# A transformer layer with a routed MoE on one core: x2 kept in SBUF, a third down buffer elsewhere, a refill in quarters, a 32-row expert last, row gathers split

## The chip, the cores and the metric

One core of one Trainium2 chip. The metric is device microseconds of one execution, lower is better. Engines: TensorE (PE), VectorE (DVE), ScalarE (ACT), GpSimd (POOL) and SyncE (SP). SP, ACT and POOL issue the DMAs of this kernel.

## The reference, cut to what matters

One layer over 512 tokens of width 1024 in float32. The mixer half (four kinds of heads and an output projection) gives `x2`. The second half is a mixture of 16 experts (4 groups of 4). A token takes its best group, and in it its two best experts:

```
h  = adaLN(rms_norm(x2), c)
p_group = softmax(h @ w_rg + b_rg);  g = argmax(p_group)
p_exp   = softmax(logits of the 4 experts of group g); two best: e1, e2
y  = p_group[g] * sum over e in (e1, e2) of p_e/(p_e1+p_e2) * ((silu(h @ w_gate[e]) * (h @ w_up[e])) @ w_down[e])
x3 = x2 + gate(c) * y;   out = rms_norm(x3) * final_norm
```

Each expert has w_gate and w_up of 1024 x 512 and w_down of 512 x 1024, 2 MB each, so the 16 experts are 96 MB of weights that each pass through SBUF once. Which tokens an expert gets is known only after the routing.

## The kernel before, in words

The first 390 us (mixer, attention, delta rule) are not touched by the change. Four output projections (L1131), one per 128 tokens, give `x2` [128, 4, 1024] in SBUF. From each block DVE makes the normalised rows `xn2`, which SP stores to HBM (`xn2_rows`, L931), and PE the 20 routing logits.

**Routing (dve_moe, pe_moe).** DVE picks group and experts by a long chain of small linked operations, up to `chosen` (tokens x experts, L1351). PE forms each token's rank within its expert with one matmul by `before` and four by `ones` (L1187, L1191). DVE turns the ranks of experts 0 and 1 into one-hot rows (`in_row`, L1359), PE multiplies both by the token numbers (L1198), and DVE copies both token lists at once (L1369). Then DVE orders the other experts by their number of tokens: `size` is an expert's position. After that come the first row of each position's tile in the output buffer (`tile0`), the surplus tiles beyond an expert's own, and the slot of each token in `expert_rows` (L1371 to L1428).

**Experts.** Position n of the run works on `ORDER[n]`. The tile heights by position in the ordering are `SIZES` = 8 of 128 rows, 4 of 64, 4 of 32. The order in which the tiles run is 0, 1, 2, 15, 3, 14, 4, 13, 5, 12, 6, 11, 7, 8, 9, 10: the last three have 64 rows. Up to 12 extra tiles of 128 rows, taken only if an expert has too many tokens, follow behind `If`s (`extras`). Each expert is: POOL gathers its rows from `xn2_rows` (L1491); PE transposes them (L987); ACT and DVE scale them into `xgT` (L1059, L1089); PE does gate and up (L1018 for 128 rows, L1012 for fewer); ACT the silu (L1066), DVE the product `hidm` (L1097, L1099); PE transposes it (L1026), ACT copies it to `hidT` (L1071); PE does down (L1049, L1044); DVE multiplies by the gate into the one buffer `yo` (L1114, L1110) and ACT stores it to `expert_rows` (L1081). DVE writes `yo` of expert n only when all stores of expert n-1 have landed. On PE the order is: hidden transposes of n-1, gate and up of n, row transposes of n+1, down of n-1. On ACT the store of expert n-1 comes before the copy of the next `hidT`.

**Weights.** Three buffers each: `gu0` to `gu2` (gate and up, 4 MB) and `dn0` to `dn2` (down, 2 MB). SP issues the loads in program order: gu0 and gu1 during attention, dn0 and dn1 after the last output projection, then the four stores of `x2` to HBM (L936), gu2, and dn2 behind a wait for those stores, as `dn2` lies on the memory of `x2`. From then on the buffer of expert n is refilled when expert n is done with it: for n = 3 to 15 gate and up wait for `gu_mm` (L952 in the file, shown as L896, the helper that issues them), down for `dn_mm` (L899). At the end SP loads `fnb` and then `x2` back from HBM as `x3` (L961).

**Tail.** When the last expert's rows have landed, POOL passes the 12 `If`s of the extra tiles and gathers the rows of each token: `y1` and `y2` in turn for the four token blocks (L1512). DVE adds `w1 * y1` (L1467) and `w2 * y2` (L1468) into `x3`, block after block, with the final norm of a block (L1478) after the next block's two additions. ACT gives the sums of squares and roots (L1285, L1287), SP stores the four blocks (L973).

```
ORDER = list(range(NBUF))
big, less = list(range(NBUF, BIG)), list(range(BIG, E))
rest = less[::-1] if NBUF == 3 else less
while big:
    ORDER.append(rest.pop(0))
    ORDER.append(big.pop(0))
ORDER += rest[::-1] if NBUF == 3 else rest
```

Of the kernel before, what the change touches and what calls it, by code (L numbers as in the profile page):

```python
# [32 lines left out]
for _n, _w in IN_SIZES.items():  # L33
# [17 lines left out]
ROUTING = {"chosen": 1, "first_rows": 2, "second_rows": 3, "first_list": 4, "experts": 5, "places": 6, "slots": 7,  # L51
           "list": 8, "w12": 9, "route_i": 10}
ROUTING_PE = {"rank_mm": 1, "first_list_mm": 2, "list_mm": 3}
SIZES = [128] * 8 + [64] * 4 + [32] * 4
TILE_START = [sum(SIZES[:n]) for n in range(E + 1)]
TILE_START += [TILE_START[E] + P * (n + 1) for n in range(EXTRA - 1)]
ROWS = TILE_START[-1] + P
# [19 lines left out]
def sbuf_map(nc):  # L77
# [55 lines left out]
    at("dn2", R1 + 64 * K + 256, [P, FT, D])  # L133
    at("x3", RW + 16 * K, [P, ST, D])
# [44 lines left out]
    for n, shape in (("lg", [P, ST, 20]), ("mx", [P, ST]), ("mn", [P, ST]), ("m1", [P, ST]), ("ed", [P, ST]),  # L179
                     ("t4", [P, ST, 4]), ("eg", [P, ST, 4]), ("ohg", [P, ST, 4]), ("oh1", [P, ST, 4]),  # L180
                     ("oh2", [P, ST, 4]), ("le", [P, ST, 4]), ("e16", [P, ST, E]), ("s16", [P, ST, E]),
                     ("M1", [P, ST, E]), ("M2", [P, ST, E]), ("chosen", [P, ST + 1, E]), ("rank", [P, ST, E]),
# [21 lines left out]
    o = at("idf", o, [P, P])  # L204
# [14 lines left out]
    o = at("vc", o, [P, HD])  # L219
    o = at("wr", o, [P, KT, 20])  # L220
# [24 lines left out]
def build(nc, A, out):  # L245
# [623 lines left out]
    x2_d = nc.dram_tensor("x2_rows", [S, D], F32).ap()  # L869
# [7 lines left out]
    big, less = list(range(NBUF, BIG)), list(range(BIG, E))  # L877
# [23 lines left out]
    def sync_moe(sp):  # L901
# [33 lines left out]
        for i in range(ST):  # L935
            sp.dma_start(x2_d[i * P:(i + 1) * P, :], T["x2"][:, i, :]).then_inc(sem("x2_st"), 16)  # L936
# [6 lines left out]
        sp.wait_ge(sem("x2_st"), 16 * ST)  # L943
        load_down(sp, 2, 2)
        sp.wait_ge(sem("routing"), ROUTING["experts"])
        expert = {}
        for n in range(NBUF, E + 1):

            if n < E:
                at_rank = 1 + EXTRA + ORDER[n]  # L950
                expert[n] = sp.value_load(T["route_i"][0:1, at_rank:at_rank + 1], min_val=0, max_val=E - 1)
                sp.wait_ge(sem("gu_mm"), n - NBUF + 1)  # L952
                load_gate_up(sp, expert[n], n % NBUF)
# [6 lines left out]
        sp.wait_ge(sem("dn_mm"), E - 2)  # L960
        sp.dma_start(T["x3"][:], x2_d.rearrange("(i p) d -> p i d", p=P)).then_inc(sem("x3_in"), 16)  # L961
# [9 lines left out]
        for i in range(ST):  # L971
            sp.wait_ge(sem("final"), i + 1)
            sp.dma_start(out[0, i * P:(i + 1) * P, :], T["x3"][:, i, :]).then_inc(sem("out_st"), 16)  # L973
# [26 lines left out]
    def pe_gate_up(pe, n, b):  # L1000
        w_in = gu[buffer_of(n)]
        pe.wait_ge(sem(f"gu_in{buffer_of(n)}"), 32 * loads_of(n))
# [114 lines left out]
    def extras(eng, body):  # L1117
# [30 lines left out]
    def pe_moe(pe):  # L1148
# [34 lines left out]

        pe.wait_ge(sem("routing"), ROUTING["chosen"])
        ch = T["chosen"]
        rank = PS[6][:, 0:(ST + 1) * E]
        t.matmul(rank, T["before"][:], ch[:].rearrange("p i e -> p (i e)"), start=True, stop=False)  # L1187
        for i in range(1, ST + 1):

            n = ST + 1 - i  # L1190
            ins = t.matmul(PS[6][:, i * E:(ST + 1) * E], T["ones"][:], ch[:, 0:n, :].rearrange("p i e -> p (i e)"),  # L1191
                           start=False, stop=(i == ST))
        ins.then_inc(sem("routing_pe"), 1)

# [1219 lines left out]
```

## Time and profile before

| | us |
|---|---|
| median of 3 runs | 793.02 (789.85, 793.02, 796.32) |
| the profiled execution | 793.18 |
| its span, first to last instruction | 791.3 |
| outside the span | 1.88 |
| PE busy in the span | 683.7 (86%) |
| DVE, ACT, POOL busy | 313.4, 179.5, 118.3 |
| HBM read, written | 159.21 MB, 18.36 MB |

All times of the trace are microseconds from the span's start. A DMA's duration in the timeline is the time to issue it; its landing is told separately. "Granted clock" is TensorE's clock as a share of full speed (1.00 is 2.4 GHz, 0.50 is 1.2 GHz). A row `x16` in the timeline is 16 neighbouring instructions; a float32 matmul shows as two.

### The profile page before, as it was taken

How to read it: one execution, taken by the hardware profiler on the slowest of the kernel's cores; microseconds unless marked ns; L12 is line 12 of the kernel's file. 1: busy time of each engine (PE TensorE's matmuls, PEld its weight loads, DVE VectorE, ACT ScalarE, POOL GpSimd, SP SyncE). 2: the span in 40 equal slices, each digit the busy share in tenths (PEclk: the TensorE clock that was granted, in tenths of full speed). 3: DMA queues.
4: the chain of work that ended last, by engine and by line, in shares of the span. 5: the costliest groups of instructions: out<-in, count | busy, mean ns of one | idle time of the engine just before them, and what ended most of it. 6: DMA issues, size and time to landing. Idle time of an engine off the chain costs nothing.

```text
span 791.3 us, 9785 instructions
## 1 busy us (share of the span) xinstructions
PE 683.7 (86%) x3805; PEld 397.5 (50%) x3809; DVE 313.4 (40%) x730; ACT 179.5 (23%) x434; POOL 118.3 (15%) x164
## 2 busy tenths in 40 slices
PE   2699899999999998889999953999999999899720
PEld 1574446667675797555544443444454454344200
DVE  3203757767566433776522256331211111111107
ACT  3204225121111212456411141111121121111103
POOL 8600123213050273000000001000000000000031
PEclk9789999999999999889999965999999999999965
DMA  9999003983320302640261099168999999999945
GB/s 332 375 261 348 3 0 107 278 253 107 107 106 1 56 2 96 183 202 1 73 194 53 28 335 382 72 277 328 407 407 426 404 398 422 370 411 411 411 164 223
DMA packets 74065, 178.31 MB, mean 225 GB/s; under 512 B 21954, under 2 KB 38940, under 8 KB 69916
## 3 DMA queue, kind: packets, MB, share of 16 engines
q1 hardware_dynamic: 67968, 161.78, 55.8%
q0 software_dynamic: 2816, 9.96, 3.4%
q10 hardware_dynamic: 3228, 5.84, 2.0%
q8 instruction: 36, 0.59, 0.3%
q14 instruction: 17, 0.14, 0.1%
HBM read 159.21 MB, written 18.36 MB: 224 GB/s over the span
## 4 chain that ended last, share of the span: by engine, by line
PE 69%; DMA 11%; DVE 9%; POOL 4%; ACT 3%; issue 3%; SPq 1%; POOLq 0%; ACTq 0%; DVEq 0%
PE ps L1018 13%; DMA gu<-in_w_up 9%; PE ps L1131 7%; PE ps L2239 7%; PE ps L2206 5%; PE ps L1049 4%; PE ps L1012 3%; PE ps L2317 2%; PE ps L2323 2%; PE ps L2203 2%; PE ps L2230 2%; PE ps L1044 2%; POOL lev L1587 2%; PE ps L2327 2%; PE ps L652 1%
## 5 line engine op out<-in xcount | busy, mean ns | idle before, releaser
L1018 PE MATMUL ps<-gu,xgT 128*128 128x512 f32 x256 | 116.0, 612 | 5.1 <-ACT xgT L1059 2.8
L1018 PEld LDWEIGHTS ps<-gu,xgT 128*128 128x128 f32 x256 | 49.7, 197 | 67.4 <-issue 64.8
L1491 POOL DMA_INDIRECT xg<-xn_rows,list x16 | 14.9, 930 | 387.1 <-PE ps L987 181.6
L2239 PE MATMUL ps<-hT,winr 128*128 128x512 f32 x144 | 72.3, 610 | 0.2
L1049 PE MATMUL ps<-dn,hidT 128*128 128x512 f32 x128 | 56.5, 594 | 0.0
L1131 PE MATMUL ps<-wout,yT 128*128 128x512 f32 x128 | 55.9, 595 | 0.0
L1692 POOL TENSOR_TENSOR cc<-low,lev 128x512 f32<-128x512 f32 x20 | 30.2, 1517 | 129.5 <-DVE low L2026 104.1
L1830 DVE SCALAR_TENSOR_TENSOR acc<-ada,st,acc 128x512 f32<-128x512 f32 x56 | 48.5, 866 | 1.3
L1012 PE MATMUL ps<-gu,xgT 128*32 128x256 f32 (+1 forms) x384 | 43.0, 452 | 2.2 <-DMA gu<-in_w_up 2.2
L2206 PE MATMUL ps<-hT,wind 128*128 128x512 f32 x96 | 42.3, 593 | 0.0
L1099 DVE TENSOR_TENSOR hidm<-sg,ps 128x512 f32<-128x512 f32 x8 | 5.5, 686 | 90.3 <-ACT sg L1066 90.3
L1131 PEld LDWEIGHTS ps<-wout,yT 128*128 128x128 f32 x128 | 24.0, 190 | 28.9 <-issue 28.9
L1049 PEld LDWEIGHTS ps<-dn,hidT 128*128 128x128 f32 x128 | 23.7, 190 | 26.9 <-issue 26.8
L1066 ACT ACTIVATE sg<-ps 128x512 f32<-128x512 f32 (+2 forms) x16 | 7.4, 464 | 128.0 <-PE ps L1018 102.5
L2239 PEld LDWEIGHTS ps<-hT,winr 128*128 128x128 f32 x144 | 23.8, 190 | 14.3 <-issue 12.3
L1012 PEld LDWEIGHTS ps<-gu,xgT 128*32 128x32 f32 (+1 forms) x384 | 16.7, 119 | 24.5 <-issue 17.2
L1114 DVE TENSOR_TENSOR yo<-ps,g2m 128x512 f32<-128x512 f32 x16 | 10.3, 686 | 46.4 <-PE ps L1049 27.8
L2125 PE MATMUL ps<-ada,st 128*32 128x128 f32 x256 | 11.6, 347 | 19.1 <-DMA ada<-in_w_ada 18.0
L1059 ACT ACTIVATE xgT<-ps,st 128x128 f32<-128x128 f32 (+2 forms) x64 | 21.9, 423 | 27.1 <-PE ps L987 26.6
L2206 PEld LDWEIGHTS ps<-hT,wind 128*128 128x128 f32 x96 | 17.8, 190 | 20.2 <-issue 20.1
L726 DVE TENSOR_REDUCE st<-ps 128x1 f32<-128x256 f32 (+3 forms) x48 | 20.3, 452 | 18.3 <-PE ps L659 18.1
L1071 ACT ACTIVATE hidT<-ps 128x512 f32<-128x512 f32 (+2 forms) x16 | 7.4, 464 | 86.6 <-DVE yo L1114 59.8
(414 smaller groups left out, 1054.2 us busy)
## 6 DMA issues: line engine op xcount, KB each, us to landing
gu<-in_w_gate SPq DMA_DIRECT2D x16, 2048.0 KB, 17.2
gu<-in_w_up SPq DMA_DIRECT2D x16, 2048.0 KB, 22.3
dn<-in_w_down SPq DMA_DIRECT2D x16, 2048.0 KB, 25.2
ada<-in_w_ada SPq DMA_DIRECT2D x12, 2048.0 KB, 11.7
expert_rows<-zero SPq DMA_DIRECT2D x12, 512.0 KB, 7.1
expert_rows<-yo ACTq DMA_DIRECT2D x8, 512.0 KB
wout<-in_w_out SPq DMA_DIRECT2D x1, 3072.0 KB, 10.6
x<-in_x SPq DMA_DIRECT2D x2, 1024.0 KB, 6.7
```

The costliest lines, as they stand in the source:

```text
L726: ins = v.tensor_reduce(m, PS[n][:, 0:nk], AX.X, ALU.max, negate=True)
L1012: ins = nc.tensor.matmul(PS[2 * b][m * s:m * s + m, 0:2 * f].rearrange("p (w f) -> p w f", w=2), T["xgT"][:, k, 0:m], w_in[:, :, k, s * f: ...
L1018: ins = nc.tensor.matmul(PS[2 * b + w][:, :], T["xgT"][:, k, :], w_in[:, w, k, :], start=(k == 0), stop=(k == KT - 1))
L1044: ins = nc.tensor.matmul(PS[4][m * w:m * w + m, 0:d], T["hidT"][:, c, m * s:m * s + m], w_in[:, f, w * d:(w + 1) * d], start=(f == 0), sto ...
L1049: ins = nc.tensor.matmul(PS[4 + w][:, :], T["hidT"][:, f, :], w_in[:, f, w * 512:(w + 1) * 512], start=(f == 0), stop=(f == FT - 1))
L1059: ins = nc.scalar.activation(T["xgT"][:, k, 0:m], PS[6][:, k * m:(k + 1) * m], ACT.Identity, scale=rA[:, k:k + 1], bias=rshift[:, k:k + 1])
L1131: ins = nc.tensor.matmul(PS[2 * (i % 2) + n][:, :], T["yT"][:, k, i * P:(i + 1) * P], T["wout"][:, k, n * 512:(n + 1) * 512], start=(k == ...
L1587: link(g.affine_select(out=t, in_=t, pattern=pattern, compare_op=op, fill=fill, base=base, channel_multiplier=cm))
L1692: g.tensor_tensor(CC[lv % 2][:], T["low"][:], T["lev"][:, lv].unsqueeze(1).broadcast_to([P, H, P]), ALU.mult).then_inc(sem("cc"), 1)
L1830: ins = v.scalar_tensor_tensor(o, piece[:, k, :], csil[:, k:k + 1], o, ALU.mult, ALU.add)
L2206: ins = t.matmul(bank[:, :], w(k), T["hT"][:, k, :], start=(k == 0), stop=(k == KT - 1))
L2239: ins = t.matmul(bank[:, :], w(k), T["hT"][:, k, :], start=(k == 0), stop=(k == KT - 1))
```

## The change

- `x2` stays in SBUF: it isn't stored to HBM nor loaded back, the tail works on it in place. `dn2` moves to memory of constants and buffers that are dead by then, and is loaded right behind dn0 and dn1, after the last output projection.
- The first refill of gate and up (buffer 0, for n = 3) comes in four parts of two k-steps each, each when expert 0's matmuls have passed these steps. 8 DMAs instead of 2.
- The order of the tiles ends with one of 32 rows: 0, 1, 2, 14, 3, 13, 4, 12, 5, 11, 6, 10, 7, 9, 8, 15. So positions 9 and 15 of the run have 64 and 32 rows where they had 32 and 64. The tile of the last expert stands at the end of `expert_rows`, which takes two more DVE operations in the routing.
- DVE forms `earlier` (chosen experts summed over earlier blocks, four linked additions), and PE forms the ranks with two matmuls instead of five.
- The lists of expert 0 and 1 go into two banks with a signal each, and POOL's gather for expert 0 waits for the first list alone.
- For a token one of whose experts is the last one, `y1` and `y2` and their weights are exchanged where needed so that `y1` never lies in the last tile. The four `y1` gathers wait only for the stores of the first 15 experts, and stand ahead of the extras' `If`s; the four `y2` gathers come last. DVE adds all four `w1 * y1` when all four have landed, then goes on by blocks with `w2 * y2`.

```diff
+OTHER_ROWS = sum(SIZES[:E - 1]) + P * EXTRA
+TILE_START += [OTHER_ROWS] + [sum(SIZES[:E - 1]) + P * n for n in range(EXTRA)]
...
-    at("dn2", R1 + 64 * K + 256, [P, FT, D])
-    at("x3", RW + 16 * K, [P, ST, D])
+    at("dn2", o2, [P, FT, D])
...
-    rest = less[::-1] if NBUF == 3 else less
+    big, less = list(range(NBUF, BIG)), list(range(E - 2, BIG - 1, -1))
     while big:
-        ORDER.append(rest.pop(0))
+        ORDER.append(less.pop(0))
         ORDER.append(big.pop(0))
-    ORDER += rest[::-1] if NBUF == 3 else rest
+    ORDER += less + [E - 1]
...
                 for b in range(2):
                     load_down(sp, b, b)
+                sp.wait_ge(sem("yo_zero"), 16 * EXTRA)
+                load_down(sp, 2, 2)
...
-        for i in range(ST):
-            sp.dma_start(x2_d[i * P:(i + 1) * P, :], T["x2"][:, i, :]).then_inc(sem("x2_st"), 16)
         sp.wait_ge(sem("g2_moved"), 1)
...
         load_gate_up(sp, 2, 2)
-        sp.wait_ge(sem("x2_st"), 16 * ST)
-        load_down(sp, 2, 2)
...
+                if n == NBUF:
+                    for part in range(4):
+                        if part < 3:
+                            sp.wait_ge(sem("first_gu_mm"), part + 1)
+                        else:
+                            sp.wait_ge(sem("gu_mm"), 1)
+                        ks = slice(2 * part, 2 * part + 2)
+                        for w, view in enumerate((wg_v, wu_v)):
+                            sp.dma_start(gu[0][:, w, ks], view[expert[n]][:, ks]).then_inc(sem("gu_in0"), 16)
+                else:
+                    sp.wait_ge(sem("gu_mm"), n - NBUF + 1)
+                    load_gate_up(sp, expert[n], n % NBUF)
...
-        sp.wait_ge(sem("dn_mm"), E - 2)
-        sp.dma_start(T["x3"][:], x2_d.rearrange("(i p) d -> p i d", p=P)).then_inc(sem("x3_in"), 16)
...
         t.matmul(rank, T["before"][:], T["chosen"][:].rearrange("p i e -> p (i e)"), start=True, stop=False)
-        for i in range(1, ST + 1):
-            n = ST + 1 - i
-            ins = t.matmul(PS[6][:, i * E:(ST + 1) * E], T["ones"][:], ch[:, 0:n, :].rearrange("p i e -> p (i e)"),
-                           start=False, stop=(i == ST))
-        ins.then_inc(sem("routing_pe"), 1)
+        t.matmul(rank, T["ones"][:], T["earlier"][:].rearrange("p i e -> p (i e)"), start=False,
+                 stop=True).then_inc(sem("routing_pe"), 1)
...
+        link(v.tensor_tensor(T["chosen"][:, 0:ST], T["M1"][:], T["M2"][:], ALU.add))
+        for i in range(1, ST + 1):
+            ins = v.tensor_tensor(T["earlier"][:, i, :], T["earlier"][:, i - 1, :], T["chosen"][:, i - 1, :], ALU.add)
...
-        v.tensor_copy(T["list"][:, 0:2], PS[5][:, 0:2]).then_inc(sem("routing"), 1)
+        v.tensor_copy(T["list"][:, 0:1], PS[4][:, 0:1]).then_inc(sem("routing"), 1)
+        dve.wait_ge(sem("routing_pe"), ROUTING_PE["second_list_mm"])
+        v.tensor_copy(T["list"][:, 1:2], PS[5][:, 0:1]).then_inc(sem("routing"), 1)
...
+        link(v.tensor_scalar(t16, order, E - 1.5, float(OTHER_ROWS - sum(SIZES[:E - 1])), ALU.is_gt, ALU.mult))
+        link(v.tensor_tensor(tile0, tile0, t16, ALU.add))
...
+        swap, move = T["mx"][:], T["mn"][:]
+        link(v.tensor_scalar(t16, order, float(LAST), None, ALU.is_equal))
+        link(v.tensor_tensor(T["s16"][:], T["M1"][:], t16.unsqueeze(1).broadcast_to([P, ST, E]), ALU.mult))
+        link(v.tensor_reduce(swap, T["s16"][:], AX.X, ALU.add))
+        for one_of, two in ((w1, w2), (T["slotf"][:, 0, :], T["slotf"][:, 1, :])):
+            link(v.tensor_tensor(move, two, one_of, ALU.subtract))
+            link(v.tensor_tensor(move, move, swap, ALU.mult))
+            link(v.tensor_tensor(one_of, one_of, move, ALU.add))
+            link(v.tensor_tensor(two, two, move, ALU.subtract))
+        v.tensor_copy(T["slot"][:], T["slotf"][:]).then_inc(sem("routing"), 1)
...
+        dve.wait_ge(sem("y1_in"), 16 * ST)
+        with dve.If(n_extra > 0):
+            dve.wait_ge(sem("y1_in"), 2 * 16 * ST)
+        for i in range(ST):
+            x = T["x2"][:, i, :]
+            ins = v.scalar_tensor_tensor(x, T["y1"][:, i, :], w1[:, i:i + 1], x, ALU.mult, ALU.add)
+        link(ins)
...
-                link(v.scalar_tensor_tensor(x, y, w1[:, c], x, ALU.mult, ALU.add))
...
+        pool.wait_ge(sem("routing"), ROUTING["slots"])
+        pool.wait_ge(sem("yo_st"), 16 * STORED[E - 1])
+        for i in range(ST):
+            rows_back(0, "y1_in", i)
+        n_extra = extras(pool, extra)
+        with pool.If(n_extra > 0):
+            pool.wait_ge(sem("y1_in"), 16 * ST)
+            for i in range(ST):
+                rows_back(0, "y1_in", i)
         pool.wait_ge(sem("yo_st"), 16 * STORED[E])
-        pool.wait_ge(sem("routing"), ROUTING["slots"])
-        extras(pool, extra)
         for i in range(ST):
-            for n, y in enumerate(("y1", "y2")):
-                g.indirect_dma_start(T[y][:, i, :], None, yo_d,
-                                     at(ap=T["slot"][:, n, i:i + 1], axis=0)).then_inc(sem(f"y_in{i}"), 16)
+            rows_back(1, f"y_in{i}", i)
```

## Rows read from the trace of the kernel before

**Rows 1.** The page, part 2: DMA's busy tenths in 40 slices of 19.8 us.
```profile
DMA  9999003983320302640261099168999999999945
```

**Rows 2.** The chain that ended last: start, length, engine and operation.
```profile
480.37 8.50 DMA xg<-xn_rows,list
492.58 16.80 PE ps L1018 x32
...
705.06 32.94 DMA gu<-in_w_up
...
757.56 2.87 DMA expert_rows<-yo
```

**Rows 3.** Windows of 5 us: busy time by engine, granted clock, DMA share, GB/s.
```profile
500.00:505.00 5.00, 5.00 (x13) 2.16 (x12) 0.00 (x0) 0.00 (x0) 0.00 (x0) 1.00 0.00 0
520.00:525.00 5.00, 5.00 (x13) 2.16 (x12) 0.00 (x0) 0.00 (x0) 0.00 (x0) 1.00 0.54 220
545.00:550.00 5.00, 5.00 (x19) 2.20 (x17) 0.00 (x0) 0.38 (x1) 0.00 (x0) 1.00 0.55 225
740.00:745.00 5.00, 5.00 (x26) 1.62 (x24) 0.00 (x0) 0.00 (x0) 0.00 (x0) 1.00 1.03 413
```

**Rows 4.** Timeline of the routing: start, length, engine, line, idle before it.
```profile
461.64 0.34 SPq L931 DMA_DIRECT2D xn_rows<-xn  x1
471.70 0.71 PE L1187 MATMUL ps<-chosen,before 128*128 128x80 f32 x2 [6.13 <-DVE chosen L1351]
472.21 1.81 PE L1191 MATMUL ps<-chosen,ones 128*128 128x64 f32 x8
475.32 3.57 PE L1198 MATMUL ps<-tok,in_row 128*128 128x1 f32 x16 [1.30 <-DVE in_row L1359]
479.35 0.16 DVE L1369 CAST list<-ps 128x2 uint32<-128x2 f32 x1 [2.28 <-PE ps L1198]
487.99 0.06 DVE L1408 MEMSET yo<- 128x1 f32 x1
```

**Rows 5.** Groups by line, 452 to 792 us: a small DVE operation, mean 175 ns.
```profile
L1441 DVE TENSOR_SCALAR t<-incl 128x16 f32<-128x16 f32 x12 | 2.1, 175 | 0.4
```

**Rows 6.** DMA issues, 455 to 475 us: size, us to landing.
```profile
xn_rows<-xn SPq DMA_DIRECT2D x1, 512.0 KB, 9.7
```

**Rows 7.** Timeline of PE in the experts: down and gate/up by rows.
```profile
640.34 1.93 PE L1044 MATMUL ps<-dn,hidT 128*32 128x256 f32 x32
...
642.79 3.66 PE L1012 MATMUL ps<-gu,xgT 128*32 128x256 f32 x64
...
671.21 7.09 PE L1012 MATMUL ps<-gu,xgT 128*64 128x512 f32 x32
...
688.75 15.70 PE L1018 MATMUL ps<-gu,xgT 128*128 128x512 f32 x32 [2.34 <-DMA gu<-in_w_up]
...
735.36 0.44 PE L1026 MATMUL ps<-idf,hidm 128*128 128x128 f32 x2
...
750.98 5.27 PE L1044 MATMUL ps<-dn,hidT 128*64 128x512 f32 x16 [2.04 <-ACT hidT L1071]
```

**Rows 8.** Timeline, stores of `yo` and the tail (first row: ACT, a 32-row expert).
```profile
586.07 1.75 ACTq L1081 DMA_DIRECT2D expert_rows<-yo  x4
...
725.39 0.34 ACTq L1081 DMA_DIRECT2D expert_rows<-yo  x1
...
736.37 0.69 DVE L1110 TENSOR_TENSOR yo<-ps,g2s 128x512 f32<-128x512 f32 x1 [3.26 <-DMA expert_rows<-yo]
...
763.76 0.94 POOL L1512 DMA_INDIRECT y<-expert_rows,slot  x1 [57.50 <-issue]
...
771.22 1.72 POOL L1512 DMA_INDIRECT y<-expert_rows,slot  x1 [0.31 <-issue]
772.16 1.28 DVE L1468 SCALAR_TENSOR_TENSOR x<-y,w2t,x 128x1024 f32<-128x1024 f32 x1
```

**Rows 9.** The tile `y`: time from issue to landing of its 8 gathers.
```profile
DMA to landing us min/median/max: 4.3/5.9/6.7
```

More of the change, by code:

```diff
@@ L50 @@
 NBUF = 3
-ROUTING = {"chosen": 1, "first_rows": 2, "second_rows": 3, "first_list": 4, "experts": 5, "places": 6, "slots": 7,
-           "list": 8, "w12": 9, "route_i": 10}
-ROUTING_PE = {"rank_mm": 1, "first_list_mm": 2, "list_mm": 3}
+ROUTING = {"before_tile": 1, "first_rows": 2, "second_rows": 3, "first_list": 4, "second_list": 5, "experts": 6,
+           "places": 7, "list": 8, "w12": 9, "slots": 10, "route_i": 11}
+ROUTING_PE = {"rank_mm": 1, "first_list_mm": 2, "second_list_mm": 3, "list_mm": 4}
 SIZES = [128] * 8 + [64] * 4 + [32] * 4
-TILE_START = [sum(SIZES[:n]) for n in range(E + 1)]
-TILE_START += [TILE_START[E] + P * (n + 1) for n in range(EXTRA - 1)]
-ROWS = TILE_START[-1] + P
+TILE_START = [sum(SIZES[:n]) for n in range(E - 1)]
+OTHER_ROWS = sum(SIZES[:E - 1]) + P * EXTRA
+TILE_START += [OTHER_ROWS] + [sum(SIZES[:E - 1]) + P * n for n in range(EXTRA)]
+ROWS = OTHER_ROWS + SIZES[E - 1]
 BIG = SIZES.count(P)
@@ L219, in sbuf_map @@
     o = at("vc", o, [P, HD])
+    o = at("acc1", o, [P, 512])
+    o = at("wpool", o, [P, 2, HD])
+    at("dn2", o2, [P, FT, D])
+    assert o2 + 16 * K <= o
+    o = at("idf", o, [P, P])
+    o = at("cols", o, [P, P])
+    o = at("ones", o, [P, P])
+    o = at("before", o, [P, P])
     o = at("wr", o, [P, KT, 20])
@@ L1001, in pe_gate_up @@
         w_in = gu[buffer_of(n)]
-        pe.wait_ge(sem(f"gu_in{buffer_of(n)}"), 32 * loads_of(n))
+        pe.wait_ge(sem(f"gu_in{buffer_of(n)}"), 32 * loads_of(n) + (96 if n >= NBUF and not buffer_of(n) else 0))
         pe.wait_ge(sem("xgT_a"), n + 1)
@@ L1314, in dve_moe @@
         lg = T["lg"]
-        link(v.memset(T["chosen"][:, ST, :], 0.0))
+        v.memset(T["chosen"][:, ST, :], 0.0)
+        link(v.memset(T["earlier"][:, 0, :], 0.0))
         link(v.tensor_tensor(T["rb"][:], T["rb"][:], PS[7][:, 80:100], ALU.add))
@@ L1455, in extra @@
             dve_output(dve, n)
-        extras(dve, extra)
+        n_extra = extras(dve, extra)
+        dve.wait_ge(sem("y1_in"), 16 * ST)
[4 more added lines that the diff above has]
+            ins = v.scalar_tensor_tensor(x, T["y1"][:, i, :], w1[:, i:i + 1], x, ALU.mult, ALU.add)
+        link(ins)
         dve.wait_ge(sem("fn_in"), 16)
-        dve.wait_ge(sem("x3_in"), 16)
-        dve.wait_ge(sem("routing"), ROUTING["w12"])
         for i in range(ST + 1):
@@ L1472, in dve_moe @@
             i -= 1
[L1473 removed]
+            c, x = slice(i, i + 1), T["x2"][:, i, :]
             dve.wait_ge(sem("ss"), 2 * ST + i + 1)
@@ L1494, in pool_moe @@
         for n in range(E):
-            if n == 2:
-                pool.wait_ge(sem("routing"), ROUTING["list"])
+            if n in (1, 2):
+                pool.wait_ge(sem("routing"), ROUTING[("second_list", "list")[n - 1]])
             if n >= 2:
```

48 lines of the change are left out of this document (23 added, 25 removed).

## The prediction, made before the changed kernel ran

> **What bounds the kernel now.** I read the page's slices first [rows 1]: in the last third, from about 545 us on, the DMA row stands at nine tenths or more until slice 38, while before it there are idle slices. The chain that ended last [rows 2] says the same in other words. It runs over PE from 492.58 on, and in the last hundred microseconds over two waits for gate/up weights, of which the longer shown takes 32.94 us and ends at 738.0, where PE starts the last expert's gate/up. From there on it is a plain sequence: the last expert, its store, the row gathers, the final norm. The windows [rows 3] date the start of the saturation: DMA is at share 0.00 in 500 to 505, at 0.54 in 520 to 525, at 0.55 in 545 to 550, and then full. The third window's end is where expert 2's gate/up matmuls end and free their buffer. So there are three stretches. (1) Up to about 550 the time goes by the routing and by PE on experts 0 to 2. (2) From 550 to 738 DMA moves weights without a gap at some 413 GB/s [rows 3]. (3) From 738 to 791.3 comes the tail of 53.3 us. What moves the start of (1) moves all behind it, since the stream of (2) starts when PE has freed the buffers; inside (2) only bytes count; in (3) each step counts.
>
> **Stretch 1: the routing.** The five rank matmuls take 471.70 to 474.02 [rows 4]. Two of width 80 take 0.71 plus about 0.45 (a quarter of the 1.81 us of the other four): 1.16 instead of 2.32, so 1.16 less. Against this DVE adds four linked additions of 175 ns [rows 5], with the link about 0.21 each: 0.84 more. Net 0.3 earlier. Bounds: 1.2 earlier to 0.8 later.
>
> The first list is the larger part. The matmuls of both lists run 475.32 to 478.89, the first list's half ends at 477.1, less the 0.3 is 476.8. DVE copied both lists 0.46 after PE's end [rows 4]; now it copies the first at 477.3, and is free by then. POOL's gather started 1.0 after that copy did (480.37 after 479.35), so now at 478.3, 2.1 earlier. If its landing takes the 8.5 us of before [rows 2], all follows 2.1 earlier, and PE starts expert 0 at 490.5 instead of 492.58.
>
> Two things stand close behind. DVE must also have finished its chain before it scales expert 0's rows: it did at 488.05 [rows 4]. Now the chain starts 0.3 earlier, has one more copy and two more linked operations (0.42 and 0.2), and so ends at 488.3. The rows' transposes would end at about 488.8, so DVE doesn't bind yet, but caps the gain at 2.1 + 0.6 = 2.7. The other is the `xn2` store. It was issued at 461.64 and took 9.7 us [rows 4, 6], so landed at 471.3, behind dn0 and dn1 (4.2 MB). Now dn2, 2.1 MB, stands ahead of it as well: 2.1 MB at 413 GB/s is 5.1 us, landing at 476.4, still ahead of the first gather at 478.3 with 1 to 2 us to spare. gu2's load moves from 471.4 to 476.5 behind it and is not needed before expert 2. It shares the DMA engines with the gather as the backlog did before, which is why I keep 8.5; without any backlog it could be the 4.3 to 6.7 of [rows 9], and then the DVE cap of 2.7 holds. Value 2.1 earlier, bounds 2.7 earlier to 2 later.
>
> The trace shows the `xn2` store at 9.7 us behind two loads of its queue [rows 6]. The Trainium skill (DMA: Bandwidth & Descriptors, section Queues, rings and completion order) says that each engine takes its descriptors of one queue in ring order and takes turns between queues. The trace agrees. By this rule the store waits for all of dn2, which is the 5.1 us above; by a free sharing of the engines it would be nothing, and both leave the gather where it is.
>
> **Stretch 2: the stream.** The refill in quarters starts gu's first refill when 2 of 8 k-steps are done, some 12 us earlier. That fills the window that shows share 0.00 [rows 3], but nothing waits for this load: the next refill waits for expert 1's matmuls, dn3 for expert 0's down, and DMA is idle again at 520 to 525 and 545 to 550. I cost it at nothing; what hides it is that idle time. Bounds: 0 to 1 gained. Its six extra issues lie on SP while SP has nothing else to issue. The four stores of `x2` lay ahead of the gather, in time that the routing covers; the load of `x3` was issued at the very end of the stream, behind all weights. So the 4.2 MB saved shorten no part of (2). The stream's end, the last gate/up load, moves by stretch 1 alone: 738.04 - 2.1 = 735.9.
>
> PE must not be later than that. Position 9 of the run now has 64 rows: 7.09 against 3.66 for gate/up [rows 7], and for down 3.65 or so (five sevenths of 5.27, of which a part ran at 1.2 GHz) against 1.93. That is 5.2 us more. PE waited 2.34 us before position 12 [rows 7] and 2.24 us before position 15 (from 735.8 to 738.04). The first wait absorbs 2.3, so position 12 starts 2.9 later; it ran 15.70 with a part at the lower clock after its wait, which without the wait falls away, some 1.8. PE is then ready for position 15 at 735.8 + 2.9 - 1.8 - 2.1 = 734.8, before the weights. If the clock part stays, it is 736.6, 0.7 after them. I take 0, bounds 0 to 0.8 lost.
>
> **Stretch 3: the tail.** Times are from the new 735.9. Gate/up of 32 rows takes 3.66, to 739.5. The down weights of the expert before land 2.1 MB later, 5.1 us, at 741.0: a new wait of 1.5. Down of 64 rows, 3.65: 744.7. DVE could write `yo` at 744.9, but needs the previous store landed. Such a store was issued at 725.39, and DVE waited for it until 736.37 [rows 8]: 11 us in the full stream. The one in question is issued at about 736.4, so lands by that at 747.4; but the stream behind it has only 5 MB left. I take the middle, 746.2 (bounds 744.9 and 747.4). Then 0.69 for DVE, some 1.1 for ACT's two issues (four take 1.75 [rows 8]), an estimated 0.3 for `hidT`: 748.4. Down of 32 rows takes 1.93 at full clock [rows 7]; the last one of before ran 5.27 after a wait of 2.04 where 3.65 is the full-speed value, so I take 3.4 (bounds 1.9 and 3.9): 751.8. DVE and the four issues of 1.75 [rows 8] bring 754.1, and 2.87 more to land [rows 2]: 757.0.
>
> `y1` needs the store of the expert before, issued by 748.0 and landed about 750.4. So POOL starts `y1` at 750.8. Each gather takes 0.94 and a gap of 0.3 [rows 8]: 755.8. Then the 12 `If`s. They cost 763.76 - 760.43 = 3.3 us on the path before [rows 2, 8] and stand now between `y1` and `y2`: `y2` starts at 759.1, after the last store (757.0). Its first block lands 5.9 later [rows 9], 765.0. All four `y1` have landed 3.7 + 5.9 = 9.6 after the first issue, 760.4; DVE adds them in 4 x 1.28 = 5.1 [rows 8]: 765.6. So DVE binds, narrowly. Block 0 is ready at 765.6 + 1.3 = 766.9; before it was 772.16 + 1.28 = 773.44 [rows 8]. From there 17.86 us remained. Two of the following steps had a `w1` product inside, 2 x 1.28 = 2.6 less (the third overlaps ACT's table load and roots): 15.3. The span ends at 782.2. Over all: stretch 1 gives 2.1, the tail 53.3 - 46.3 = 7.0. With the 1.9 outside the span, 784.1, against 793.18 of the profiled run, which is the median of 793.02.
>
> Before, one gather took 1.72 instead of 0.94 while DVE added rows [rows 8]. The Trainium skill (SBUF — State Buffer, section Who interferes with whom) says that a DVE instruction with two SBUF inputs and a GpSimd instruction that reads SBUF exclude each other. By it each `y2` gather issued under the four `w1` products may take up to 1.3 more; by most rows it takes nothing. DVE uses a block only every 3 us, so the last block would be late by under 1 us in the worst case.
>
> DVE's 12 operations for the exchange of weights and slots (2.5 us) fall in the stretch before the silu of expert 1, where DVE is idle, as in 520 to 525 [rows 3]. If that cover were gone, expert 1's product would be late by as much. Bounds 0 to 1.
>
> **The rivals.**
> - *The front gives nothing.* The `xn2` store lands later than 478 behind dn2, or the gather meets gu2's load at its densest. For it: a slack of only 1 to 2 us. Against: 5.1 us is all that dn2 holds. The gather lands 1 us later than before: 784.1 + 3.1 = 787.2.
> - *More than forecast.* The stream gains from the early refill, or the gather lands early, or the store of position 13 lands in time. For it: 1.3 us in that store, 0.6 at the DVE cap, 1.6 if `y1` lands in 4.3 [rows 9]. Against: PE can start the last expert only at 734.8, so the stream can give 1.1 at most. Time 781.
> - *Slower: the split gathers hang on a late store.* Each store of `yo` lands 11 us after its issue [rows 8] even as the stream runs out, one behind the other. Then the store of position 14 is issued from 748.1 to 749.2 and lands at 760.5; `y1` starts at 761 instead of 750.8, and the three serial pieces behind it (9.6, 5.1 and 16.6 us) end the span at 792.3, time 794.2, 1 us slower than before. It decides from a start of `y1` at 759.9 on. Against: the stream is empty from about 747, and a store in empty queues took 2.87 [rows 2].
> - *PE binds in the stream* by position 9's 64 rows: 784.9, within the forecast's own range.
>
> **How the numbers follow.** The forecast 784.1 has 0.50 with its own range 781.5 to 787; the front gives nothing 0.17; more than forecast 0.23; the late store 0.06; 0.04 for what I don't see. The bounds of the parts add to 780.6 at best, and with the scatter of the runs to 778.5; upwards to the first rival and some of the third, 790.5. About 1% (785.1) is what a measurement can tell from no change. Below it lie six tenths of the forecast's case, nearly all of the better one: 0.55 faster. The late store alone is within 1%; slower by more takes it together with the lost front (797), or what I don't see: 0.04. Within: 0.41.
>
> **What would show it.** Right: the first gather issued near 478 and expert 0's matmuls near 490.5; a refill between 494 and 508 with DMA idle again before 525; saturation from about 548; gate/up of the last expert near 736; `y1` gathers from about 751 and `y2` about 3.3 us after their end; four additions in a row on DVE. Wrong: a wait of the first gather for `xn_rows`; last weights landing well ahead of 735; `y1` starting after 757; a wait of PE at position 10 or 13 that was not there.

## The result, and the profile after

The changed kernel takes 786.75 us (median of 20 runs, 782.02 to 790.91), the kernel before 792.61 (20 runs of its own beside it). The ratio is 0.9919 with a 95% interval of 0.9898 to 0.9941: 0.8% faster, 5.9 us. The forecast was 784.1 with a range of 778.5 to 790.5. The profiled execution has a span of 785.7, 5.6 less than before. In the experiments below two single runs took far longer, 1750.54 us in experiment 1 and 1402.13 us in experiment 3, and the ratios leave them out.

The page of the changed kernel, its slices of DMA and its HBM traffic:

```profile
DMA  9999003973330302640161077438999999999964
...
HBM read 157.12 MB, written 16.26 MB: 221 GB/s over the span
```

2 MB less are read and 2 MB less written, so `x2` really stays on the chip. The saturated slices are the same ten as before.

Where the 5.6 us went needs an anchor, since the mixer part, which no kernel here touches, ends up to 6 us apart from one execution to the next. I use M, the start of DVE's `memset` of `chosen` at the head of the routing, and L, the start of the last expert's gate/up. Expert 0's first matmul is e0. From the timelines, with the span of each:

| | M | first gather issued | its rows in | DVE's chain done | e0 | L - e0 | span - L |
|---|---|---|---|---|---|---|---|
| before | 465.64 | M+14.73 | M+23.27 | M+22.35 | M+26.94 | 245.46 | 53.26 |
| changed | 464.73 | M+12.35 | M+24.45 | M+22.16 | M+28.12 | 245.19 | 47.66 |

("Its rows in" is the moment when PE can start to transpose them.) So the front lost 1.2 instead of gaining 2.1, the stream is the same to 0.3, and the tail gained 5.6. The other 0.9 is M itself and says nothing of the change, to which 4.7 of the profile's 5.6 are left.

The front in the timeline of the changed kernel (rows 4 are those of before):

```profile
454.98 1.49 SPq L899 DMA_DIRECT2D dn<-in_w_down  x3
...
460.72 0.34 SPq L933 DMA_DIRECT2D xn_rows<-xn  x1
...
471.64 0.72 PE L1196 MATMUL ps<-chosen,before 128*128 128x80 f32 x2 [6.99 <-DVE earlier L1359]
472.15 0.64 PE L1197 MATMUL ps<-earlier,ones 128*128 128x80 f32 x2
...
475.00 0.34 SPq L896 DMA_DIRECT2D gu<-in_w_gate  x1
475.38 0.43 SPq L896 DMA_DIRECT2D gu<-in_w_up  x1
...
476.06 0.16 DVE L1380 CAST list<-ps 128x1 uint32<-128x1 f32 x1 [0.22 <-PE ps L1203]
477.08 1.17 POOL L1521 DMA_INDIRECT xg<-xn_rows,list  x1 [175.27 <-DVE list L1380]
...
486.88 0.06 DVE L1422 MEMSET yo<- 128x1 f32 x1
...
489.18 1.97 PE L994 MATMUL ps<-idf,xg 128*128 128x128 f32 x8 [11.52 <-DMA xg<-xn_rows,list]
```

The rank step is shorter and the first list is copied as soon as it is there: the gather is issued 2.4 earlier, counted from M. But gu2's load now goes out at 475.00, 2.1 us ahead of the gather, where it had gone out at 471.40, 9 us ahead. The gather takes 12.1 instead of 8.5, and PE waits 11.52 for it.

Windows of the changed kernel, columns as in rows 3:

```profile
500.00:505.00 5.00, 5.00 (x13) 2.28 (x12) 0.00 (x0) 0.00 (x0) 0.00 (x0) 1.00 0.83 258
...
520.00:525.00 5.00, 5.00 (x13) 2.28 (x12) 1.93 (x12) 0.00 (x0) 0.00 (x0) 1.00 0.00 0
...
545.00:550.00 5.00, 5.00 (x16) 2.09 (x15) 0.00 (x0) 0.16 (x1) 0.00 (x0) 1.00 0.61 247
```

The early refill fills 500 to 505, which had share 0.00, and empties 520 to 525, which had 0.54. It moved idle time and took none away.

The end of the chain that ended last, of the changed kernel:

```profile
706.27 31.73 DMA gu<-in_w_up
738.04 3.66 PE ps L1019 x64
741.70 1.98 issue
743.68 5.37 PE ps L1053 x16
750.33 2.37 DMA expert_rows<-yo
753.44 0.94 POOL y L1533
757.18 6.96 DMA y<-expert_rows,slot
```

The last expert's gate/up takes 3.66. The 1.98 named "issue" is the wait for the down weights of position 14 that the forecast had as new. The down behind it takes 5.37. From there the chain passes through position 14's store and the `y1` gathers, not through the last expert's down or its stores.

The tail in the timeline of the changed kernel:

```profile
751.33 1.93 PE L1053 MATMUL ps<-dn,hidT 128*32 128x256 f32 x32 [2.03 <-ACT hidT L1080]
...
753.44 0.94 POOL L1533 DMA_INDIRECT y<-expert_rows,slot  x1 [46.02 <-DMA expert_rows<-yo]
...
761.59 0.94 POOL L1533 DMA_INDIRECT y<-expert_rows,slot  x1 [3.48 <-DMA expert_rows<-yo]
...
764.37 4.87 DVE L1490 SCALAR_TENSOR_TENSOR x<-y,w1t,x 128x1024 f32<-128x1024 f32 x4 [10.56 <-DMA y<-expert_rows,slot]
```

`y1` starts at L+15.4 and `y2` at L+23.55. DVE begins the four `w1` products when the last `y1` has landed, L+26.3, and they decide when block 0 goes on.

### The profile page after: what moved, and what is told of

It reads as the page before. It is cut to its first block, busy times and chain, and to the rows that moved or that the text cites. A ratio compares the mean times of both kernels' runs of the same rounds, so it can differ in the third digit from the quotient of the medians.

```text
span 785.7 us, 9804 instructions
## 1 busy us (share of the span) xinstructions
PE 681.1 (87%) x3799; PEld 396.2 (50%) x3803; DVE 317.3 (40%) x749; ACT 180.1 (23%) x434; POOL 117.9 (15%) x165
## 4 chain that ended last, share of the span: by engine, by line
PE 74%; DVE 8%; DMA 7%; POOL 4%; ACT 3%; issue 3%; POOLq 0%; ACTq 0%; SPq 0%; DVEq 0%
PE ps L1025 14%; PE ps L1141 7%; PE ps L2281 7%; PE ps L1058 6%; PE ps L2248 5%; DMA gu<-in_w_up 4%; PE ps L1019 4%; PE ps L2359 2%; PE ps L2365 2%; PE ps L2245 2%; PE ps L1053 2%; PE ps L2272 2%; POOL lev L1629 2%; PE ps L653 2%; PE ps L2369 2%
## 5 line engine op out<-in xcount | busy, mean ns | idle before, releaser
L1025 PE MATMUL ps<-gu,xgT 128*128 128x512 f32 x256 | 114.1, 605 | 2.8 <-ACT xgT L1068 2.8
L1521 POOL DMA_INDIRECT xg<-xn_rows,list x16 | 14.9, 930 | 390.7 <-PE ps L994 182.6
L1141 PE MATMUL ps<-wout,yT 128*128 128x512 f32 x128 | 57.6, 609 | 0.0
L1058 PEld LDWEIGHTS ps<-dn,hidT 128*128 128x128 f32 x128 | 23.7, 190 | 26.9 <-issue 26.8
L1053 PE MATMUL ps<-dn,hidT 128*32 128x256 f32 (+1 forms) x192 | 24.0, 474 | 4.0 <-ACT hidT L1080 2.0
```

The lines of the kernel that those rows point to most:

```text
L1053: ins = nc.tensor.matmul(PS[4][m * w:m * w + m, 0:d], T["hidT"][:, c, m * s:m * s + m], w_in[:, f, w * d:(w + 1) * d], start=(f == 0), sto ...
L1058: ins = nc.tensor.matmul(PS[4 + w][:, :], T["hidT"][:, f, :], w_in[:, f, w * 512:(w + 1) * 512], start=(f == 0), stop=(f == FT - 1))
L1141: ins = nc.tensor.matmul(PS[2 * (i % 2) + n][:, :], T["yT"][:, k, i * P:(i + 1) * P], T["wout"][:, k, n * 512:(n + 1) * 512], start=(k == ...
```

## The experiments

A ratio is always to the kernel before, run beside the experiment. Its median was 794.75 beside experiments 1, 2, 4 and 5, 793.00 beside 6 to 9 and 796.35 beside 3 and 10, so medians of different groups are not to be compared directly. Each experiment has 4 to 12 runs and one profile.

**1. hold_gu2: is it gu2's load that slows the gather?**

```diff
+        sp.wait_ge(sem("xg_in0"), 16)
         load_gate_up(sp, 2, 2)
```

> The changed kernel, but gu2's load is issued only when expert 0's rows have landed. In the changed kernel the first gather was issued at 477.08, 2 us behind this load, and took 12.06 us, landing with the load (489.2). Theory: the gather lands when the weight bytes issued just ahead of it have passed; then it takes 4.3 to 7 us here, expert 0 waits for DVE's chain (ends at 486.9) instead, its matmuls start near 488.5 instead of 492.85, the weight stream's end moves from 738.0 to about 734, and the time is 4 us under that of the changed kernel (ratio to before 0.987). Rival: the gather is slow because DVE's small operations hold up POOL's descriptors; then it still takes 11 to 12 us and the time is that of the changed kernel (0.992). Second rival: the front is shorter but the stream or PE takes it back; then matmuls start early and the last gate/up still starts at 738.

Its timeline:

```profile
481.56 1.18 POOL L1522 DMA_INDIRECT xg<-xn_rows,list  x1 [177.07 <-DVE list L1381]
...
486.16 1.97 PE L995 MATMUL ps<-idf,xg 128*128 128x128 f32 x8 [4.01 <-DMA xg<-xn_rows,list]
486.19 0.35 SPq L896 DMA_DIRECT2D gu<-in_w_gate  x1
...
491.37 0.06 DVE L1424 MEMSET yo<- 128x1 f32 x1
```

The gather took 4.6 us. DVE's operations are the same, so the rival with the descriptors falls. e0 is M+23.72, 4.4 earlier than in the changed kernel, and bound by DVE's chain, which ends 5.2 after the rows are in. L - e0 is 245.67, so the gain was not taken back by the stream. The ratio to before is 0.985 (0.980 to 0.990) against 0.9919: in the right direction, though the intervals of the two just touch.

**2. hold_up_half: all of the load, or what is ahead of the gather?** Only the up half waits; the gate half goes out as before.

```diff
-        load_gate_up(sp, 2, 2)
+        sp.dma_start(gu[2][:, 0], wg_v[2]).then_inc(sem("gu_in2"), 16)
+        sp.wait_ge(sem("xg_in0"), 16)
+        sp.dma_start(gu[2][:, 1], wu_v[2]).then_inc(sem("gu_in2"), 16)
```

> As the run that holds gu2, but only its up half (2 MB) is held until expert 0's rows have landed; the gate half is issued at 475.0 as in the changed kernel. Theory that the gather lands with the bytes ahead of it: 2 MB are 5.1 us less, so it takes about 7 us and lands near 484, and expert 0 starts at DVE's cap near 488.5, as with all of gu2 held. Rival, the gather gets a fixed share of busy engines: it takes 8 to 10 us as in the stream (median 9.4). Time 3 to 4 us under the changed kernel by the first, 2 to 3 by the second.

The gather took 6.8 us with 2 MB issued 2.6 us ahead of it, the 7 of the first theory and not the 8 to 10 of the other; e0 at M+23.73, DVE's cap again. Ratio 0.984 (0.980 to 0.987), median 781.45.

Its timeline, in the tail, where a `y2` gather met DVE's `w1` products:

```profile
755.83 4.87 DVE L1492 SCALAR_TENSOR_TENSOR x<-y,w1t,x 128x1024 f32<-128x1024 f32 x4 [9.39 <-DMA y<-expert_rows,slot]
755.95 1.98 POOL L1535 DMA_INDIRECT y<-expert_rows,slot  x1 [0.30 <-issue]
```

The gather was issued 0.12 us into the first product, which takes 1.28 us. It took 1.98 instead of 0.94 and ended 0.8 after that product did.

**3. dn2_late: which part of the change did it?**

```diff
                 for b in range(2):
                     load_down(sp, b, b)
-                sp.wait_ge(sem("yo_zero"), 16 * EXTRA)
-                load_down(sp, 2, 2)
...
         load_gate_up(sp, 2, 2)
+        sp.wait_ge(sem("yo_zero"), 16 * EXTRA)
+        load_down(sp, 2, 2)
```

> The changed kernel, with one edit: dn2's load stands behind gu2's again instead of behind dn0 and dn1 (x2 stays in SBUF). Theory (it was dn2 ahead of the xn2 store that spoiled the front): the store lands 5 us earlier, gu2 is issued near M+5.7 instead of M+10.3 (M: the routing's first memset), so most of it has passed when the gather is issued at M+12.35; rows land in 8 to 9 us instead of 12, the matmuls start at M+24.5 to M+25 instead of M+28, and the time is 3 us under the changed kernel (ratio to before 0.988). Rival (the gather is slow behind any weight load of 4 to 6 MB under way, whenever it was issued): 12 us again, the changed kernel's 0.992.

Its timeline:

```profile
470.06 0.34 SPq L896 DMA_DIRECT2D gu<-in_w_gate  x1
...
476.79 1.18 POOL L1521 DMA_INDIRECT xg<-xn_rows,list  x1 [175.22 <-DVE list L1380]
...
485.54 1.97 PE L994 MATMUL ps<-idf,xg 128*128 128x128 f32 x8 [8.17 <-DMA xg<-xn_rows,list]
```

The `xn2` store landed in 9.5 us, against 14.2 in the changed kernel, gu2 went out at M+5.6, the gather took 8.75, and e0 is M+24.77: 3.35 earlier than in the changed kernel and 2.2 earlier than before. That is the front's gain that was forecast, and the early dn2 had taken it. Ratio 0.984 (0.980 to 0.988), 782.30. The profile is 6.6 under the changed kernel's; the front explains 3.35 of it, a tail without the step of TensorE's clock that experiment 7 is about another 2.4.

**4. no_quarters.** The first refill as one gate and one up load after `gu_mm`.

```diff
-                if n == NBUF:
+                if False:
...
-        pe.wait_ge(sem(f"gu_in{buffer_of(n)}"), 32 * loads_of(n) + (96 if n >= NBUF and not buffer_of(n) else 0))
+        pe.wait_ge(sem(f"gu_in{buffer_of(n)}"), 32 * loads_of(n))
```

> The changed kernel, with the first refill as one gate and one up load after all of expert 0's gate/up matmuls, as before. Theory: nothing waits for this load, as the next refill waits for expert 1's matmuls; DMA is idle after it anyway: the same time within 0.3 us in the trace, last gate/up at 738. Rival: the early refill shortens the stream; then this costs 2 to 8 us.

L - e0 is 244.76 against 245.19, so the refill in quarters gives nothing that can be seen. Ratio 0.990 (0.986 to 0.994), the changed kernel's own.

**5. before_order: the order of the tiles alone, in the kernel before.**

```diff
-    rest = less[::-1] if NBUF == 3 else less
+    rest = less[:-1][::-1]
...
-    ORDER += rest[::-1] if NBUF == 3 else rest
+    ORDER += rest + [E - 1]
```

> The kernel before, with one part of the change alone: the order of tiles ends with the 32-row one, position 9 has 64 rows. Theory: gate/up of the last expert 3.4 us shorter, of which 1.9 go into a wait for the down weights of the expert before; its four stores cost 1 us more in issuing; the y gathers start 2 to 3 us earlier than 763.8, and the rest is as before: time 2 to 3 us under before (ratio 0.997). Rival: PE's 5.2 us more at position 9 make PE the bound of the stream: no gain or up to 2 us slower.

Its timeline:

```profile
744.97 1.10 ACTq L1081 DMA_DIRECT2D expert_rows<-yo  x2
...
746.45 1.93 PE L1044 MATMUL ps<-dn,hidT 128*32 128x256 f32 x32 [2.04 <-ACT hidT L1071]
751.67 0.42 DVE L1110 TENSOR_TENSOR yo<-ps,g2q 128x256 f32<-128x256 f32 x1 [6.73 <-DMA expert_rows<-yo]
```

PE was done with the last expert at 748.4, but DVE could write the one `yo` buffer only at 751.67, when position 14's store had landed. The tail is 52.67 instead of 53.26, the ratio 0.998 (0.995 to 1.0005): by itself the 32-row expert gives at most little. I had expected 2 to 3 us and had left this wait out. PE's 64 rows at position 9 cost nothing (L - e0 244.44), so the rival falls too.

**6. x3_load: does the 2 MB load at the end of the stream matter?** The changed kernel with such a load put back.

```diff
+        sp.wait_ge(sem("dn_mm"), E - 2)
+        sp.dma_start(dn[1][:], A["x"][0].rearrange("(i p) d -> p i d", p=P)).then_inc(sem("x3_in"), 16)
```

> The changed kernel, plus a 2 MB load (of x, into dn1's memory, read by nobody) where the kernel before loaded x3. In the run with the order alone DVE waited for the 13th position's neighbour store: a store of yo issued at 744.97 took 6.7 us to land while this load ran. Theory: the last weights start at the same time, but the stores of position 14 land 3 to 4 us later, y1 starts at L+18 to L+19 instead of L+15.4, and the tail is 3 us longer (ratio to before 0.996). Rival: the 2 MB pass behind everything and cost nothing, the time is the changed kernel's 0.992.

Its timeline:

```profile
748.37 1.10 ACTq L1094 DMA_DIRECT2D expert_rows<-yo  x2
...
754.97 0.42 DVE L1123 TENSOR_TENSOR yo<-ps,g2q 128x256 f32<-128x256 f32 x1 [6.63 <-DMA expert_rows<-yo]
...
755.59 0.94 POOL L1537 DMA_INDIRECT y<-expert_rows,slot  x1 [48.18 <-DMA expert_rows<-yo]
```

The wait of 6.6 for position 14's store is back, as in experiment 5, and `y1` starts at L+17.4 instead of the L+13.5 of the runs whose down of position 14 ran as fast as here (3.65). L - e0 is 244.93, so the stream is no longer. The tail is 48.7, against 44.8 to 45.3 in experiments 2 to 4. Ratio 0.995 (0.993 to 0.998) against 0.9919 (0.9898 to 0.9941): the intervals overlap a little, and it is the trace that shows the cause. So with this order of tiles `x2` on the chip is worth some 3 us, not by its bytes in the stream but by an empty queue for the last stores.

**7. warm: what the waits do to TensorE's clock.** Two unused matmuls in each of PE's last two waits.

```diff
+            else:
+                for w in range(2):
+                    t.matmul(PS[7][:, :], T["ones"][:], gu[0][:, w, 0, :], start=True, stop=True)
...
         pe_hidden(pe, E - 1, 1)
+        for w in range(2):
+            t.matmul(PS[7][:, :], T["ones"][:], gu[0][:, w, 0, :], start=True, stop=True)
```

> The changed kernel, plus two unused 128x512 matmuls on PE in each of its last two waits: after the last gate/up (wait 1.98 for the down weights of position 14) and after its hidden transposes (wait 2.03 for hidT). In the changed kernel's profile the down matmuls of position 14 ran 5.35 at a granted clock near 0.57, in two others 3.65 at 1.00. Theory: the wait brings the clock down; without it down of position 14 runs 3.65, and the tail is 45 to 46 instead of 47.7. Rival: the clock falls regardless of that wait, or the extra matmuls delay the down by as much as they save: tail 46 to 49. The time can't tell 1 us; the trace can.

A window of the changed kernel:

```profile
744.00:746.00 2.00, 2.00 (x8) 0.77 (x6) 0.00 (x0) 0.00 (x0) 0.00 (x0) 0.55 1.04 422
```

and of this one:

```profile
742.00:744.00 2.00, 2.00 (x12) 0.79 (x10) 0.00 (x0) 0.00 (x0) 0.00 (x0) 1.00 1.03 417
```

The downs ran 3.65 and 1.93 at a granted clock of 1.00 (2.4 GHz), where the changed kernel had 5.35 for the first at 0.55, near the level of 1.2 GHz. But of the ten profiles without the filling, three (experiments 3 to 5) had no such step either, and the other seven had it at the one down or the other, the kernel before among them [rows 7]. So the two with the filling and without a step, this one and experiment 10, are a hint and no proof. The time, 784.41 with a ratio of 0.990 (0.986 to 0.993), can't tell.

**8. split_late: the gathers not split.** All four `y1` behind the last stores and the extras' Ifs, then the `y2`.

```diff
-        pool.wait_ge(sem("yo_st"), 16 * STORED[E - 1])
+        pool.wait_ge(sem("yo_st"), 16 * STORED[E])
+        n_extra = extras(pool, extra)
         for i in range(ST):
             rows_back(0, "y1_in", i)
-        n_extra = extras(pool, extra)
```

> The changed kernel, with the y1 gathers and the extras' Ifs behind the last expert's stores, all four y1 ahead of the four y2. Counted from the start of the last expert's gate/up (L): stores landed at L+21, Ifs 3.3, y1 starts at L+24.3 instead of L+15.4, y2 follows 5 later, y1 has landed at L+34, DVE's four products end at L+39, the span ends near L+54.5. Theory (the split is the tail's main gain): the tail is 54 to 55 instead of 45 to 47.7, the time 7 to 9 us above the changed kernel (ratio to before 1.002). Rival (the gain is of the 32-row expert and of x2 in SBUF; the gathers' landing binds either way): 2 to 4 us above it.

Its timeline:

```profile
760.96 0.95 POOL L1533 DMA_INDIRECT y<-expert_rows,slot  x1 [54.32 <-issue]
...
771.68 3.68 DVE L1490 SCALAR_TENSOR_TENSOR x<-y,w1t,x 128x1024 f32<-128x1024 f32 x3 [18.81 <-DMA y<-expert_rows,slot]
```

`y1` starts at L+23.6 and the tail is 55.6, longer than before's 53.26, as DVE now waits for four blocks instead of one pair. Median 795.13, ratio 1.002 (1.000 to 1.004). So the split with its new place is worth 8 us or more to this tail; the change lives on it. The parts don't add up one by one, though: what the split gives without the 32-row expert last and without `x2` on the chip was not run.

**9. rows_early: past DVE's cap.** Experiment 1, with one more edit:

```diff
         link(v.tensor_tensor(bb, bb, tile0, ALU.subtract))
+        dve_rows(dve, 0)
         wide_pad = pad.unsqueeze(1).broadcast_to([P, ST, E])
...
         v.memset(T["yo"][:, 1:2], 0.0).then_inc(sem("yo_st"), 16)
-        dve_rows(dve, 0)
```

> The run that holds gu2 until expert 0's rows have landed, and in addition DVE scales expert 0's rows (dve_rows) 11 small operations earlier in its chain, right after bb. There DVE's chain bound the start of expert 0: rows landed 4.6 us after the gather's issue, the chain was done 22.2 us after the routing's first memset (M), matmuls started at M+23.7. Theory: DVE reaches the rows at M+19.4, their transposes end at M+18.9, so the matmuls start near M+21.1, 2.6 earlier, and the rest follows as it is: stream 245, tail 45 to 47, time 6 to 7 us under the changed kernel (ratio to before 0.983). Rival: PE at its low clock or the token lists, which now come 1.5 later, take it back.

e0 is M+20.91, 7.2 earlier than in the changed kernel, L - e0 245.74. The tail was a long one (47.8, with the down at 5.35). Ratio 0.982 (0.979 to 0.985), median 779.12. The later token lists took nothing back that shows.

**10. all_four: rows_early, warm, and a looser tail.**

```diff
-            rows_back(0, "y1_in", i)
+            rows_back(0, f"y1_in{i}", i)
...
+            dve.wait_ge(sem(f"y1_in{i}"), 16)
             x = T["x2"][:, i, :]
...
         extras(act, extra)
+        a.activation(rstd[:, 0:1], rstd2[:, 0:1], ACT.Sqrt)
```

> A version that should beat both: rows_early (gu2 held until expert 0's rows have landed, DVE scales them earlier) with warm's unused matmuls, and in the tail a signal for each y1 block, so that DVE adds w1*y1 as the blocks land, and ACT loads its table for the roots ahead of the sums (one unused root). Theory: front M+20.9 as in rows_early; down of position 14 and 15 at 3.65 and 1.93; DVE's w1 products end 1.3 after the last y1 block, near L+26, so the y2 block (L+28 to L+29) binds instead of L+31.2; the table saves 1.3 more; tail 42 to 43; time 5 us under rows_early (ratio to before 0.976). Rival: DVE's products and POOL's gathers hold each other up (one gather took 1.97 beside them): tail 44 to 45.

Its timeline:

```profile
754.40 1.28 DVE L1498 SCALAR_TENSOR_TENSOR x<-y,w1t,x 128x1024 f32<-128x1024 f32 x1 [4.41 <-DMA y<-expert_rows,slot]
755.19 1.28 ACT L1292 ACT_TABLE_LOAD   x1 [7.74 <-issue]
755.95 1.28 DVE L1498 SCALAR_TENSOR_TENSOR x<-y,w1t,x 128x1024 f32<-128x1024 f32 x1 [0.27 <-DMA y<-expert_rows,slot]
...
758.24 2.52 DVE L1498 SCALAR_TENSOR_TENSOR x<-y,w1t,x 128x1024 f32<-128x1024 f32 x2 [1.00 <-DMA y<-expert_rows,slot]
758.56 1.77 POOL L1541 DMA_INDIRECT y<-expert_rows,slot  x1 [0.30 <-issue]
...
762.34 1.29 DVE L1506 SCALAR_TENSOR_TENSOR x<-y,w2t,x 128x1024 f32<-128x1024 f32 x1 [1.59 <-DMA y<-expert_rows,slot]
...
765.39 1.28 DVE L1506 SCALAR_TENSOR_TENSOR x<-y,w2t,x 128x1024 f32<-128x1024 f32 x1 [1.76 <-DMA y<-expert_rows,slot]
```

The `w1` products now lie beside the gathers and DVE waits for `y2` instead: the first block by 1.59 and the second by 1.76, so the `y2` landings hold back part of what the table load gave. The rival is there in part: the second block's gather met a product and took 1.77 to issue instead of 0.94. Tail 43.75, a little over the 42 to 43 expected. Median 776.76 against 796.35 of before beside it, ratio 0.9765 (0.972 to 0.981): 2.3% faster than before, and the fastest version here.

## Why the prediction was right or wrong

- **What bounds, and the three stretches.** Right. L - e0 lay between 244.1 and 245.8 in all twelve profiles, whatever was done to the front, the order or the refill.
- **The rank step, 0.3 earlier.** Right: DVE copied the ranks at M+8.41 before and M+8.09 after (474.05 and 472.82).
- **The first gather at 478.3, 2.1 earlier.** Right in its issue: M+12.35 instead of M+14.73, 2.4.
- **"If its landing takes the 8.5 us of before".** This is the step that failed. It took 12.1. The forecast itself had gu2's load move from 471.4 to 476.5, and kept the 8.5 because gu2's load "shares the DMA engines with the gather as the backlog did before". It left out how closely ahead of the gather that load is now issued. Nothing ahead gave 4.6 us, 2 MB issued 2.6 us ahead 6.8, 4 MB issued 2.1 ahead 12.1; but 4 MB and dn2's 2 MB issued 6.7 and 5.9 us ahead 8.75. Experiments 1 to 3 show this: the front lost 1.2 us instead of gaining 2.1.
- **The `xn2` store 5.1 later.** Nearly right in size: 14.2 us to landing against 9.7 [rows 6], 4.5 more. The Trainium skill (DMA: Bandwidth & Descriptors, Queues, rings and completion order) says that on each engine a queue's descriptors are taken in ring order. The trace agrees by these 4.5 us for the dn2 ahead. The conclusion drawn from it, that either way the gather stays where it is, was wrong: the store itself had slack, but gu2's load is issued behind a wait for it and so came next to the gather.
- **DVE's cap 0.6 behind.** Right as the next bound, wrong in its place: with the gather out of the way, DVE set e0 at M+23.7 (experiments 1 and 2), which is 3.2 earlier than before and not 2.7. Its chain ended at M+22.16, where the forecast's 488.3 is M+22.66. Moving one step of it gave 2.8 more (experiment 9).
- **The refill in quarters at nothing; PE's 64 rows at position 9 at nothing.** Both right (experiments 4 and 5). PE waited 1.06 us for the last gate/up where 1.1 had been worked out.
- **The tail, 46.3.** It was 47.7 in the profile, and 44.8 to 45.3 in experiments 2 to 4, which have the same tail code and had position 14's down at 3.65. On the way to `y1` two terms were off and nearly cancelled: the store of position 13 didn't hold up position 14 (the middle value of 1.3 us was not needed), and the clock stepped down at position 14's down, 5.35 for 3.65. `y1` came at L+15.4 where I had L+14.9, and its last block took 6.96 to land instead of 5.9. These two, 1.6 together, make up the 1.4 by which the tail was longer than forecast. The clock step that I had put at the last down, 3.4, did not come (1.93).
- **The 12 Ifs, 3.3 us.** I had them between `y1` and `y2`, with the stores landed 2 us before their end. They are hidden: `y2` waited 3.48 us for stores, and in experiment 6 only 1.93, less than the Ifs' 3.3. The last expert's stores were issued by L+18.1, as forecast, but released `y2` 5.4 us later and not 2.9. So `y2` at L+23.55, where I had L+23.2, is luck: one wait took the place of another. In experiment 8, where the Ifs are on the path again, `y1` came 6.3 us after the last store had been issued (with the 2.9 to land of [rows 2], 3.4 are left for them).
- **GpSimd and DVE at the same SBUF ports.** The Trainium skill (SBUF — State Buffer, Who interferes with whom) says that a DVE instruction with two SBUF inputs contends with a GpSimd instruction that reads SBUF. From the rows I had put that at up to 1.3 us for each `y2` gather under the `w1` products. The trace agrees for gathers issued while a product is under way, one per profile in most: 1.98 instead of 0.94 in experiment 2, 1.72 in the kernel before, 1.15 in the changed one. In the changed kernel and in experiment 2 DVE waited for none of them, so it cost nothing there.
- **The rivals.** "The front gives nothing", 787.2, is what came: 786.75, and 787.40 in the profiled run. It had 0.17, and the second of its two reasons, the gather meeting gu2's load, is the true one. That 786.75 also lies within the forecast's own 781.5 to 787 is in part luck: the front was 3.3 worse and the tail 1.4 worse than forecast, and M happened to be 0.9 earlier in the profile. "More than forecast" and "late store" did not come; the late store was real only with the x3 load beside it (experiments 5 and 6). I had the better forecast of the tail and the worse one of a load that I had moved myself on paper.

## What to carry to other kernels

A load that moves later because something was put ahead of its wait can land on a transfer that is waited for; of each DMA that a change moves, write down what is issued in the few microseconds behind it. A prefetch whose data nobody waits for should be held back until the small gather on the path has landed: one wait brought expert 0's matmuls 4.4 us forward here. And what is saved in bytes may pay elsewhere than in the stream: put back into the changed kernel, a load like that of `x3` cost nothing in the stream and some 3 us in the landing of the last stores.

## What the runs showed of the hardware that I had not expected

- A 512 KB row gather took 4.6, 6.8, 8.75 and 12.1 us to land, by what weight loads were issued ahead of it and how closely. In before and in experiment 3 it landed ahead of dn2 (at 494.2 and 490.7), which had been issued 3.9 and 5.9 us before it. It landed 1.9 and 2.7 us behind gu2's up half there, and within 1 us of it where gu2 had been issued about 2 us ahead: 0.2 behind in the changed kernel, 0.8 ahead in experiment 6. Which rule decides between the two is open; the runs only rule out that the total of bytes ahead does.
- A gather that GpSimd issues while a two-input DVE product is under way ends 0.8 us after that product, however far it had come. In experiment 2 the product ended at 757.11 and the gather at 757.93; in the kernel before it was 772.12 and 772.94. All thirteen such gathers, in eleven profiles, show it. Gathers issued at the same instant as the next product (four, in experiments 1 to 4) kept their 0.94.
- The last expert's four stores of 32 KB took 2.2 us to land (the middle value) with nothing beside them (experiment 5) and 3.6 beside the `y1` gathers (experiment 10).
- Two-microsecond waits of PE were followed by a lower granted clock in some executions and not in others with the same tail code (5.35 or 3.65 for the same 16 matmul records). That is 1.7 us of this tail.
- The changed kernel's 20 runs spread over 9 us, more than the change gives. The seven runs above 789 us had a mean granted clock of 0.931 to 0.937, the other thirteen 0.937 to 0.942. Where in the kernel the clock differs was not looked at.
